# Rows of the weights' parts and of all operand buffers step by 64 bytes modulo 512

## The reference, cut to what matters

```
a = rms_norm(x, norm_mix);      y = stick_breaking(a @ w_qkv) @ w_o;   h = x + y
h = h + square(relu(rms_norm(h, norm_mlp) @ w1)) @ w2;                 x = rms_norm(h, final_norm)
h = [16 meta tokens, x];        proj = rms_norm_2(h) @ w_in            # u, gb, gc, v, ga, gbr
y_a = pooled(u) @ pool_w * pool_scale;   y_b = (gb * conv3(gc * v)) @ conv_out_w
h = h + (sigmoid(ga) * y_a + sigmoid(gbr) * y_b) @ w_o_2
h = h + (silu(g) * up) @ w_down          # g, up = split(rms_norm_2(h) @ w_gate_up)
out = rms_norm_2(h)[:, 16:]
```

## Time and profile before

| | |
|---|---|
| median of 3 runs | 2572.76 us (2572.55 to 2573.6) |
| profiled execution, first to last instruction | 2570.3 us |
| TensorE busy | 2561.2 us, 100% |
| weight loads busy | 2461.8 us, 96% |
| VectorE busy | 1578.9 us, 61% |
| ScalarE busy | 1153.0 us, 45% |

### The profile page before, as it was taken

The page is one execution under the profiler, slowest core; times in us unless marked ns, Lnnn a source line. Parts: engine busy times, 40 slices in busy tenths (PEclk is TensorE's granted clock), DMA queues, the critical chain, the costliest instruction groups (busy, mean ns, idle before and its releaser), DMA issues.

```text
span 2570.3 us, 47399 instructions
## 1 busy us (share of the span) xinstructions
PE 2561.2 (100%) x19871; PEld 2461.8 (96%) x19871; DVE 1578.9 (61%) x1343; ACT 1153.0 (45%) x1126; POOL 139.1 (5%) x87
## 2 busy tenths in 40 slices
PE   9999999999999999999999999999999999999998
PEld 9999999999999999999899988899999889998997
DVE  6577766655556556786654776566755555555555
ACT  5455554434434434544533344444444434443444
POOL 0000100000000000000200530000000000000001
PEclk9999999999999999999999999999999999999999
DMA  7554455556555565555555555555555556555563
GB/s 263 184 165 163 164 181 188 192 195 196 195 190 191 195 197 196 186 181 189 183 186 188 183 181 195 182 195 197 193 187 193 182 195 197 196 190 190 194 212 131
DMA packets 243978, 485.64 MB, mean 189 GB/s; under 512 B 7729, under 2 KB 8945, under 8 KB 243697
## 3 DMA queue, kind: packets, MB, share of 16 engines
q1 hardware_dynamic: 243520, 483.12, 56.8%
q10 hardware_dynamic: 320, 0.53, 0.1%
HBM read 481.53 MB, written 2.10 MB: 188 GB/s over the span
## 4 chain that ended last, share of the span: by engine, by line
PE 99%; DVE 0%; POOL 0%; issue 0%; ACT 0%; DVEq 0%; POOLq 0%; ACTq 0%
PE ps L1414 48%; PE ps L1422 24%; PE ps L1385 8%; PE ps L1347 8%; PE ps L1391 4%; PE ps L1357 4%; PE ps L1470 0%; PE ps L1524 0%; PE ps L1436 0%; PE ps L1458 0%; PE ps L1407 0%; PE ps L1278 0%; PE ps L1288 0%; PE ps L1529 0%; PE ps L1507 0%; PE ps L1461 0%
## 5 line engine op out<-in xcount | busy, mean ns | idle before, releaser
L790 DVE TENSOR_TENSOR wlo<-raw,whi 128x1024 fp32r<-128x1024 f32 x900 | 1138.9, 1274 | 944.1 <-ACT whi L582 943.8
L582 ACT ACTIVATE whi<-raw 128x1024 fp32r<-128x1024 f32 x900 | 949.9, 1060 | 1335.9 <-PE ps L1422 1008.4
L1414 PE MATMUL ps<-b_buf,whi 128*128 128x256 f32 x5734 | 711.5, 276 | 0.5 <-DVE za L1005 0.5
L1414 PEld LDWEIGHTS ps<-b_buf,whi 128*128 128x128 f32 x5734 | 679.6, 188 | 1.1 <-DVE za L1005 0.7
L1422 PE MATMUL ps<-b_buf,wlo 128*128 128x256 f32 x2880 | 386.3, 276 | 0.0
L1422 PEld LDWEIGHTS ps<-b_buf,wlo 128*128 128x128 f32 x2880 | 354.4, 188 | 0.0
L1414 PE MATMUL ps<-a_buf,whi 128*128 128x258 f32 (+4 forms) x2560 | 330.9, 282 | 0.0
L1414 PEld LDWEIGHTS ps<-a_buf,whi 128*128 128x128 f32 x2560 | 315.7, 188 | 0.3
L1414 PE MATMUL ps<-c_buf,whi 128*128 128x256 f32 x2542 | 314.4, 276 | 0.0
L1414 PEld LDWEIGHTS ps<-c_buf,whi 128*128 128x128 f32 x2542 | 300.4, 188 | 0.2
L1347 PE MATMUL ps<-a_buf,whi 128*128 128x512 f32 x768 | 185.7, 394 | 0.0
(11 more groups left out here) (206 smaller groups left out, 1254.4 us busy)
## 6 DMA issues: line engine op xcount, KB each, us to landing
raw<-in_mlp_w_dram SPq DMA_DIRECT2D x128, 1024.0 KB, 5.4
raw<-in_w_in_dram SPq DMA_DIRECT2D x96, 1024.0 KB, 5.1
raw<-in_w_gate_up_dram SPq DMA_DIRECT2D x88, 1024.0 KB, 5.0
raw<-in_sb_w_qkv_dram SPq DMA_DIRECT2D x44, 1024.0 KB, 5.1
raw<-in_w_down_dram SPq DMA_DIRECT2D x44, 1024.0 KB, 5.0
raw<-in_sb_w_o_dram SPq DMA_DIRECT2D x16, 1024.0 KB, 5.0
raw<-in_conv_out_w_dram SPq DMA_DIRECT2D x16, 1024.0 KB, 5.0
raw<-in_w_o_dram SPq DMA_DIRECT2D x16, 1024.0 KB, 5.0
```

Source lines behind the costliest of these rows:

```text
L582: act.activation(whi[:, unit_of(n, u)], raw[:, n % RAW, u * UK:(u + 1) * UK, :], ACT.Copy).then_inc(w_hi, 1)
L790: dve.tensor_tensor(wlo[:, s], raw[:, n % RAW, u * UK:(u + 1) * UK, :], cast(whi[:, s]), ALU.subtract).then_inc(w_lo, 1)
L1414: pe.matmul(outs[j], whi[:, s, kt, j * P:(j + 1) * P], part[:, x, tok], start=first and kt == 0 and part is hi and (alone or j % 2 == 0), ...
```

## The change

The rows of `whi` and `wlo` become 528 numbers long (2112 bytes, `PW + M`; 512 are used), and those of `b_buf`, `c_buf` and `d_buf` 272 (1088 bytes, `TW`), like those of `a_buf`. All of these rows then move by 64 bytes modulo 512 per k tile, and the ring of eight k-tile rows comes round after 512. The bases keep their distances: `a_buf` and `d_buf` at a multiple of 512 from the weights, `c_buf` and `b_buf` at 64 more; the tokens of `a_buf` begin 64 bytes into a row. To make room, the scratch `ms` and `t1` move into memory that is free at that time (`G`, and `U` to `S2`), and `pp` moves up behind the attention's other tiles. Every other edit follows from the new shapes. No instruction is added, removed or moved: each engine has as many rows in its order as before, in the same order.

```diff
-        whi, _ = place("whi", [P, SPLIT, UK, PW], F32R)
-        wlo, _ = place("wlo", [P, SPLIT, UK, PW], F32R)
+        whi, _ = place("whi", [P, SPLIT, UK, PW + M], F32R)
+        wlo, _ = place("wlo", [P, SPLIT, UK, PW + M], F32R)
         a_buf, a_off = place("a_buf", [P, 2, NT, TW], F32R)
-        c_buf, _ = place("c_buf", [P, 2, NT, T], F32R, at=a_off + 64)
-        d_buf, _ = place("d_buf", [P, 2, NT, T], F32R, at=a_off)
+        c_buf, _ = place("c_buf", [P, 2, NT, TW], F32R, at=a_off + 64)
+        d_buf, _ = place("d_buf", [P, 2, NT, TW], F32R, at=a_off)
         top[0] += 64
-        b_buf, b_off = place("b_buf", [P, 2, NT, T], F32R)
+        b_buf, b_off = place("b_buf", [P, 2, NT, TW], F32R)
...
-        ms, _ = place("ms", [P, 2, TW])
+        ms, _ = place("ms", [P, 2, TW], at=region + 26624)
...
-        t1, _ = place("t1", [P, GH, 3 * P], at=at + 16384)
-        pp, p_off = place("pp", [P, 2, GH, 3 * P], F32R, at=at + 22528)
+        t1, _ = place("t1", [P, GH, 3 * P], at=u_off + 4 * GH * 3 * P)
+        pp, p_off = place("pp", [P, 2, GH, 3 * P], F32R, at=at + 16384)
...
-                    act.activation(whi[:, unit_of(n, u)], raw[:, n % RAW, u * UK:(u + 1) * UK, :],
+                    act.activation(whi[:, unit_of(n, u), :, 0:PW], raw[:, n % RAW, u * UK:(u + 1) * UK, :],
                                    ACT.Copy).then_inc(w_hi, 1)
...
-                    dve.tensor_tensor(wlo[:, s], raw[:, n % RAW, u * UK:(u + 1) * UK, :], cast(whi[:, s]),
+                    dve.tensor_tensor(wlo[:, s, :, 0:PW], raw[:, n % RAW, u * UK:(u + 1) * UK, :], cast(whi[:, s, :, 0:PW]),
                                       ALU.subtract).then_inc(w_lo, 1)
```

More of the change, by code:

```diff
@@ L291, in build @@
         raw, _ = place("raw", [P, RAW, KT, PW])
-        whi, _ = place("whi", [P, SPLIT, UK, PW], F32R)
-        wlo, _ = place("wlo", [P, SPLIT, UK, PW], F32R)
+        whi, _ = place("whi", [P, SPLIT, UK, PW + M], F32R)
+        wlo, _ = place("wlo", [P, SPLIT, UK, PW + M], F32R)
         a_buf, a_off = place("a_buf", [P, 2, NT, TW], F32R)
-        c_buf, _ = place("c_buf", [P, 2, NT, T], F32R, at=a_off + 64)
-        d_buf, _ = place("d_buf", [P, 2, NT, T], F32R, at=a_off)
+        c_buf, _ = place("c_buf", [P, 2, NT, TW], F32R, at=a_off + 64)
+        d_buf, _ = place("d_buf", [P, 2, NT, TW], F32R, at=a_off)
         top[0] += 64
-        b_buf, b_off = place("b_buf", [P, 2, NT, T], F32R)
-        a_hi, a_lo, b_hi, b_lo = a_buf[:, 0], a_buf[:, 1], b_buf[:, 0], b_buf[:, 1]
-        c_hi, c_lo, d_hi, d_lo = c_buf[:, 0], c_buf[:, 1], d_buf[:, 0], d_buf[:, 1]
+        b_buf, b_off = place("b_buf", [P, 2, NT, TW], F32R)
+        a_hi, a_lo = a_buf[:, 0], a_buf[:, 1]
+        b_hi, b_lo = b_buf[:, 0, :, 0:T], b_buf[:, 1, :, 0:T]
+        c_hi, c_lo = c_buf[:, 0, :, 0:T], c_buf[:, 1, :, 0:T]
+        d_hi, d_lo = d_buf[:, 0, :, 0:T], d_buf[:, 1, :, 0:T]
         h, _ = place("h", [P, NT, T])
@@ L592, in split_unit @@
                     act.wait_ge(w_used, n + 1 - SPLIT)
-                act.activation(whi[:, n % SPLIT], raw[:, n // UNITS % RAW, n % UNITS * UK:(n % UNITS + 1) * UK, :],
+                act.activation(whi[:, n % SPLIT, :, 0:PW], raw[:, n // UNITS % RAW, n % UNITS * UK:(n % UNITS + 1) * UK, :],
                                ACT.Copy).then_inc(w_hi, 1)
@@ L720, in body @@
                     if st.name == "dn_2" and k == 3 and c == 0:
-                        act.activation(ms[:, 1, 0:2], ms[:, 0, 0:2], ACT.Sqrt)
+                        act.activation(stat[:, 22:24], stat[:, 2:4], ACT.Sqrt)
                     if st.name == "dn_0" and (k, c) in H_TURNS:
@@ L816, in split_unit @@
                 dve.wait_ge(w_hi, n + 1)
-                dve.tensor_tensor(wlo[:, n % SPLIT], raw[:, n // UNITS % RAW, n % UNITS * UK:(n % UNITS + 1) * UK, :],
-                                  cast(whi[:, n % SPLIT]), ALU.subtract).then_inc(w_lo, 1)
+                dve.tensor_tensor(wlo[:, n % SPLIT, :, 0:PW],
+                                  raw[:, n // UNITS % RAW, n % UNITS * UK:(n % UNITS + 1) * UK, :],
+                                  cast(whi[:, n % SPLIT, :, 0:PW]), ALU.subtract).then_inc(w_lo, 1)
             def first_panel():
@@ L1384, in chunk @@
                                 for m in range(MT):
-                                    pe.matmul(ps[:, 4 * half + m, :], part[:, x, toks[m]], whi[:, s, kt, :],
+                                    pe.matmul(ps[:, 4 * half + m, :], part[:, x, toks[m]], whi[:, s, kt, 0:PW],
                                               start=first and kt == 0 and part is hi, stop=False,
@@ L1390, in chunk @@
                             for m in range(MT):
-                                last = pe.matmul(ps[:, 4 * half + m, :], hi[:, x, toks[m]], wlo[:, s, kt, :],
+                                last = pe.matmul(ps[:, 4 * half + m, :], hi[:, x, toks[m]], wlo[:, s, kt, 0:PW],
                                                  start=False, stop=stop and kt == UK - 1, skip_group_check=True)
@@ L1523, in last_chunks @@
                             for kt in range(UK):
-                                pe.matmul(ps[:, 4 * half + m, :], part[:, x + kt, tok], whi[:, s, kt, :], start=False,
+                                pe.matmul(ps[:, 4 * half + m, :], part[:, x + kt, tok], whi[:, s, kt, 0:PW], start=False,
                                           stop=False, skip_group_check=True)
@@ L1528, in last_chunks @@
                         for kt in range(UK):
-                            last = pe.matmul(ps[:, 4 * half + m, :], d_hi[:, x + kt, tok], wlo[:, s, kt, :],
+                            last = pe.matmul(ps[:, 4 * half + m, :], d_hi[:, x + kt, tok], wlo[:, s, kt, 0:PW],
                                              start=False, stop=s == units[-1][0] and kt == UK - 1,
```

## The result

The changed kernel takes 2626.59 us (median of 4 runs, 2626.31 to 2627.29), the one before 2573.18 beside it: a ratio of 1.0209, 95% interval 1.0197 to 1.0222. It is 53.4 us slower; 2624 was forecast.

What follows compares the result with a forecast made beforehand. TensorE's matmul rate was taken to bound the kernel. Terms 52 + 0.6 + 2 = +54.6 us on the 2570.3 us span, with the median 2.5 above it, gave 2627, rounded down to 2624; range 2560 to 2634.

Steps and rivals of the forecast that it cites:

- What bounds the kernel: Whole kernel: TensorE alone, busy 2561.2 of 2570.3 us; the other engines wait for it.
- Two paces of one instruction, kept by equal addresses: 256-column matmuls: quick 113.2 ns or slow 117.8; a stream of equal addresses keeps the pace it has.
- Which weights a row meets: Large products: a moving row meets the next matmul's weights, so one in four matmuls gets a foreign distance.
- Term 1: Single 256-column matmuls on `b_buf` and `c_buf`: 11,570 quick ones lose 4.5 ns each, +52 us (bounds +13 and +52).
- Term 2: Single matmuls on `a_buf`: slow already and staying slow, 0.
- term 3: Paired chunks: 128 pairs on `b_buf` go to `a_buf`'s value, +0.6 us; `a_buf`'s 768 stay.
- Term 4: `d_buf` stationary, in dn: half of the 1,008 matmuls and the last 48 at 4 ns, +2 us.
- Term 5: ScalarE and VectorE writing longer rows: covered by idle time, 0; moved scratch changes no instruction, 0.
- Heals at once: Rival: on `b_buf` and `c_buf` streams the pace returns right after each foreign distance; 2576 us, chance 0.28.
- faster: Rival: own distance counts, or 0 and 128 are harmless, and `a_buf` streams turn quick; -26 us, 2547 us, chance 0.15.
- nothing: Rival: distances don't count anywhere and the paces come from something else that stays; 2573 us, chance 0.05.

Runs made afterwards that it cites:

- The kick: Kernel before plus three extra matmuls: in w1_0 (distance 0), gu_1 (distance 128) and gu_2 (distance 64); 2604.16 us, ratio 1.0123.
- scratch run: Kernel before with only `ms`, `t1` and `pp` moved, all rows at their lengths of before; 2599.88 us, ratio 1.0105.
- `a_buf` with its aligned rows: Kernel before with `a_buf` rows of 1280 bytes; `acc`, `ms`, `t1` moved, all other addresses modulo 512 as before; 2568.02 us, ratio 0.9983.

## Why the prediction was right, and where it was not

**What bounds the kernel**: right. The chain is all PE, and the other engines did nothing but wait longer.

**Two paces of one instruction, kept by equal addresses**: shown. The kick at distance 64 changes nothing, and those at 0 and 128 change all that follows in their stages. In the changed kernel itself the quick pace comes back twice and ends after five matmuls, at the first excursion.

**Which weights a row meets**: half right. That equal distances to the own weights don't suffice is shown by the changed kernel. That the next weights' distance alone decides isn't: with it at 64 (modulo 256) and the own at 192, 116.7 ns. The timeline hadn't excluded the own weights either. In the window of w2_0 in the kernel before:

```profile
L1414 PEld LDWEIGHTS ps<-b_buf,whi 128*128 128x128 f32 x469 | 55.4, 188 | 0.0
```

By the profile a load lasts 188 ns at a spacing of 113, so one that starts with the matmul ahead runs on for 75 ns beside its own. The count of one foreign distance in four holds for the next weights; the own ones never change in this kernel.

**Term 1**, +52: 48.7 measured. The upper bound was the right choice, and the argument for it (w_o never heals) was the right one. It was 3 us too large. By the single starts the pace came out at 117.6 ns in w1 and w2 and at 117.4 to 117.6 behind them, against 113.3: a loss of 4.1 to 4.3 ns rather than 4.5. And w_o, counted as 0, gained a little. Distances of 0 at j = 3, 115.6 ns in w1 and w2, aren't as bad inside this pattern as they are when constant, 119.8.

**Term 2**, 0, and **term 3**, +0.6: within 1 us of what the windows show (paired chunks in gb 466 for 463 matmuls, in co 206 for 207).

**Term 4**, +2: 4.3 measured. Half of the matmuls were charged 4 ns; the window shows 3.5 ns on all of them, the single starts 4.4 (231.1 for 226.7). The step that failed is that a matmul at the old distance next to one at another keeps its old time. By the starts each of the twelve places in a unit takes 228 to 237 ns on average, where each took 226 to 227: here too the pace as a whole was lost.

**Term 5**, the moved scratch at 0: wrong as an edit by itself. Alone it costs 26.7 us, all in w1 and w2, since it shifted other tensors by 384 bytes modulo 512; by what way that reaches w1_0 is open. In the whole change it adds nothing visible, because the rows take the quick pace from the same matmuls. "Changes no instruction" was no reason for 0 where addresses are what is priced. So of the 53 us, some 27 (wo2, gu, dn and co) are the rows' alone. The other 26 (w1 and w2) have two causes, each of which is enough by what the runs show. The scratch run shows the one. For the other speak the kick and w1_0 of the changed kernel, where the five wide matmuls did bring the quick pace and the first excursion ended it. The change with its other addresses aligned, which would show the rows' part by itself, wasn't run.

**The closeness of the number** is in part luck: term 1 was 3 us too large and term 4 was 2 too small. The 3 us rounded off, for matmuls that keep the quick pace behind wide ones, had no such size: they were five in each of two places, under 0.1 us.

**The rivals.** "Heals at once" is refuted by the kick, "faster" by the first windows, and "nothing" by the time. The Trainium skill, SBUF — State Buffer, section "SBUF: two separate sides", gives LDWEIGHTS a read port of its own and has TensorE wait for nobody. The runs don't show where in the chip the time goes, so they don't refute the ports. They refute what the prediction took from the rule, a sum of 0: with the distance between two operands of TensorE a matmul goes from 113.3 to 119.8 ns.

What stays open: what the two paces are inside. That a quick stream is one in which two reads keep out of each other's way is argued, not shown. Also open are whether the own distance counts by itself, whether the period is 256 bytes in every case, and which phase lets wide matmuls bring the quick pace.

## What to carry to other kernels

When TensorE is the bound and neighbours take turns between weights and a moving row, count the matmuls in windows of single stages: the same instruction at two rates, at the same clock, points to addresses. Compare distances with the weights loaded meanwhile as well as with a row's own, and keep them equal, at the value that measures best. A change that only moves other tensors should keep all addresses of what TensorE reads modulo 512; else a gain or loss of 1%, as in the scratch run, may be the move's and not the edit's.

## What was not expected of the hardware

One extra matmul of 0.28 us at the wrong distance cost some 26 us in w1 and w2. Four or five wide matmuls restored the quick pace in the kernel before and failed to do so after a shift of unrelated tensors. The constant distances order as 64 (113.3 ns when quick, 117.8 when not), 128 (118.6), 0 (119.8). Apart from `a_buf` with its aligned rows, nothing that was tried beat the distances that the kernel before already has.
